# Indexer queries projected before keys, values and queries, and the indexer's scores dealt out among the eight query projections

## What is computed

```python
(u_h, u_b, u_c, z_a, q, k, v, qi, ki, wi, z_b, g_a, g_b) = _split_proj(h @ w_in)
q = _rms(q.reshape(b, t, N_HEADS, HEAD_DIM), q_norm)          # 8 heads of 128
k = _rms(k.reshape(b, t, N_KV_HEADS, HEAD_DIM), k_norm)       # 2 heads of 128
qi = qi.reshape(b, t, N_IDX_HEADS, IDX_DIM)                   # 8 indexer heads of 64

def _index_scores(qi, wi, kidx):
    s = jnp.einsum('btid,bsd->btis', qi, kidx) * (IDX_DIM ** -0.5)
    w = wi * (N_IDX_HEADS ** -0.5)
    return jnp.einsum('btis,bti->bts', jax.nn.relu(s), w)

sc = jnp.where(key_pos <= pos, _index_scores(qib, wib, kidx), NEG_INF)
_, idx = lax.top_k(sc, 256)
```

## Time and profile before

| | us |
|---|---|
| median of 3 runs | 3638.25 |
| lowest and highest run | 3633.06, 3639.53 |
| span of the profiled execution | 3631.9 |
| PE busy | 3443.6 (95%) |
| DVE busy | 2334.5 (64%) |
| ACT busy | 1497.9 (41%) |
| POOL busy | 1561.8 (43%) |

### The profile page before, as it was taken

How to read it: one execution, slowest core, us unless ns; L and a number is a source line. 1 busy time by engine, 2 the same in 40 slices (tenths; PEclk the granted TensorE clock), 3 DMA queues, 4 the chain that set the end, 5 groups by cost and what they waited for, 6 DMA issues and landing times.

```text
span 3631.9 us, 44594 instructions
## 1 busy us (share of the span) xinstructions
PE 3443.6 (95%) x16753; PEld 2772.4 (76%) x16753; DVE 2334.5 (64%) x3959; ACT 1497.9 (41%) x2452; POOL 1561.8 (43%) x1076
## 2 busy tenths in 40 slices
PE   7899999999899999999999999979999999997999
PEld 6779888855577778887777688868877588876887
DVE  2563599200263589953546999985555999997653
ACT  2344432332353354335533643334433744334532
POOL 2226564300154438753353287541263167650014
PEclk9999999988899999999999999989999999998999
DMA  7222223343334423342244133420144133440005
GB/s 202 73 82 86 60 70 99 99 166 136 100 99 122 117 65 97 104 134 60 75 144 118 38 95 100 128 78 13 46 146 126 33 85 95 114 127 9 10 13 160
DMA packets 520871, 338.02 MB, mean 93 GB/s; under 512 B 15405, under 2 KB 494823, under 8 KB 518610
## 3 DMA queue, kind: packets, MB, share of 16 engines
q1 hardware_dynamic: 517202, 297.41, 29.6%
q0 software_dynamic: 3456, 37.75, 2.8%
HBM read 296.36 MB, written 38.76 MB: 92 GB/s over the span
## 4 chain that ended last, share of the span: by engine, by line
PE 63%; DVE 26%; issue 5%; ACT 3%; POOL 2%; DMA 1%; SPq 1%; ACTq 0%; DVEq 0%; POOLq 0%
PE ps L982 58%; DVE JUNK L1635 12%; PE ps L987 5%; DVE GE L1637 1%; DVE SC L1577 1%; DVE SMALL L1641 1%; DVE SMALL L1639 1%; DVE PFX L1661 1%; DVE SMALL L1642 1%; DVE QI L1555 1%; DVE QI L1556 1%; ACT T L673 1%; DVE RS L1510 1%; DVE BD L1664 1%; DVE SC L1665 1%
## 5 line engine op out<-in xcount | busy, mean ns | idle before, releaser
L982 PE MATMUL ps<-HTH,WLH 128*128 128x512 f32 x4672 | 1480.4, 393 | 3.2 <-POOL WLH L1858 3.2
L1858 POOL TENSOR_TENSOR WLH<-WR,WLH 128x1024 fp32r<-128x1024 f32 x388 | 957.1, 2467 | 1161.2 <-ACT WLH L582 1161.0
L982 PEld LDWEIGHTS ps<-HTH,WLH 128*128 128x128 f32 x4672 | 880.1, 188 | 192.0 <-issue 6.5
L982 PE MATMUL ps<-HTL,WLH 128*128 128x512 f32 x2336 | 911.6, 390 | 0.0
L582 ACT ACTIVATE WLH<-WR 128x1024 fp32r<-128x1024 f32 x388 | 411.4, 1060 | 1032.0 <-DMA WR<-in_w_in 753.4
L1635 DVE TENSOR_SCALAR_CACHE_REDUCE JUNK<-SC,SMALL 128x384 bf16<-128x384 f32 (+13 forms) x392 | 579.9, 1479 | 25.6 <-POOL SC L1906 10.0
L982 PEld LDWEIGHTS ps<-HTL,WLH 128*128 128x128 f32 x2336 | 440.3, 188 | 94.3 <-issue 6.5
L1708 DVE CUSTOM_DVE_ANT_0 LP<-ps,SC 128x512 f32<-128x512 f32 (+3 forms) x320 | 187.5, 609 | 226.1 <-PE ps L982 223.4
L982 PE MATMUL ps<-T,V 128*128 128x256 f32 x1088 | 283.0, 388 | 5.8 <-ACT T L858 5.8
L982 PEld LDWEIGHTS ps<-T,V 128*128 128x128 f32 x1088 | 187.0, 191 | 34.4 <-ACT T L858 12.6
L1510 DVE RECIPROCAL RS<-RS 128x512 f32<-128x512 f32 x40 | 134.1, 3352 | 107.3 <-ACT RS L657 107.2
(11 more groups left out here) (314 smaller groups left out, 5417.4 us busy)
## 6 DMA issues: line engine op xcount, KB each, us to landing
WR<-in_w_in SPq DMA_DIRECT2D x292, 512.0 KB, 3.9
WR<-in_w_proj_a SPq DMA_DIRECT2D x32, 512.0 KB, 4.1
WR<-in_w_proj_b SPq DMA_DIRECT2D x32, 512.0 KB, 4.2
WR<-in_w_out SPq DMA_DIRECT2D x32, 512.0 KB, 4.3
MW<-in_w_mod SPq DMA_DIRECT2D x24, 512.0 KB, 7.2
XN<-in_x_prompt SPq DMA_DIRECT2D x4, 2048.0 KB, 9.4
q_scratch<-QO SPq DMA_DIRECT2D x32, 256.0 KB, 4.4
ma_scratch<-T SPq DMA_DIRECT2D x32, 256.0 KB, 4.4
```

The source lines that it names most:

```text
L982: return pe.matmul(out, lhsT, rhs, start=start, stop=stop, **more)
L1858: pool.tensor_tensor(WL[j % 3][:, :, :], WR[j % 3][:, :, :], WH[j % 3][:, :, :].bitcast(F32), ALU.subtract).then_inc(*w_split.mark(j))
```

## The change

`PROJ_A` is reordered to `ki`, 4 `qi`, 2 `k`, 2 `v`, 8 `q`. The index stage's units are cut into eight equal shares (`index_share`: 2, 8, 12 or 16 units in tiles 0 to 3), and share k is issued with query head k's projection: on PE behind the products of that projection (and behind `after_a` of the one ahead), on ACT behind `root_a` of the one ahead, on DVE in front of `item_a` of that head.

```diff
-PROJ_A = [("ki", 0)] + [("k", h) for h in range(KV)] + [("v", h) for h in range(KV)] \
-    + [("q", h) for h in range(HEADS)] + [("qi", i) for i in range(IH // 2)]
+PROJ_A = [("ki", 0)] + [("qi", i) for i in range(IH // 2)] + [("k", h) for h in range(KV)] \
+    + [("v", h) for h in range(KV)] + [("q", h) for h in range(HEADS)]
+QI_LAST = PROJ_A.index(("qi", IH // 2 - 1))
+Q_FIRST = PROJ_A.index(("q", 0))
...
+    def index_share(t, i):
+        units = [(b, h, c, n) for b in index_blocks(t) for h in range(IH) for c, n in pieces(width(BLOCKS * t + b))]
+        m, k = len(units), i - Q_FIRST
+        return units[m * k // HEADS:m * (k + 1) // HEADS] if k >= 0 else []
...
                 evac_a(t, i, j)
                 if i:
                     root_a(t, i - 1)
+                index_relu(t, i)
                 j += 1
             root_a(t, len(PROJ_A) - 1)
-            index_relu(t)
...
                 if i >= 2:
                     turn_keys(t, i - 2)
+                index(t, i)
                 j += 1
             after_a(t, len(PROJ_A) - 1, j - 1)
-            index(t)
...
             for i in range(len(PROJ_A)):
+                weigh(t, i)
                 item_a(t, i, j)
                 j += 1
-            weigh(t)
```

More of the change, by code:

```diff
@@ L660, in _, with index_relu @@
         relus = [0]
[L662 to L674, removed]
+        def index_relu(t, i):
+            if i == Q_FIRST:
+                act.wait_ge(*a_done.at(t, QI_LAST, last_part(t)))
+            for b, h, c, n in index_share(t, i):
+                r = relus[0]
+                relus[0] += 1
+                act.wait_ge(*idx_done.at(t, b, h, c))
+                if r >= 4:
+                    act.wait_ge(*scored.at(r - 4))
+                act.activation(T[1 + r % 4][:, 0:n], ps[bank("idx", t, b, h, c)][:, 0:n], ACT.Relu
+                               ).then_inc(*relu.mark(r))
         def conv_taps(f):
@@ L1136, in turn_keys, with index @@
                 freed[b] = a_done.at(t, i, p)
[L1138 to L1151, removed]
+        def index(t, i):
+            if i == Q_FIRST:
+                pe.wait_ge(*a_done.at(t, QI_LAST, "P"))
+            for blk, h, c, n in index_share(t, i):
+                b = aux("idx", t, blk, h, c)
+                q = QI[:, h, blk * P:(blk + 1) * P]
+                mm(ps[b][:, 0:n], q, KIH[:, c:c + n], True, False)
+                mm(ps[b][:, 0:n], q, KIL[:, c:c + n], False, True).then_inc(*idx_done.mark(t, blk, h, c))
+                freed[b] = relu.at(relus[0])
+                relus[0] += 1
         relus = [0]
@@ L1559, in _, with weigh @@
         relus = [0]
[L1561 to L1577, removed]
+        def weigh(t, i):
+            for blk, h, c, n in index_share(t, i):
+                r = relus[0]
+                relus[0] += 1
+                dve.wait_ge(*relu.at(r))
+                dst = scores(t)[:, blk, c:c + n]
+                x = T[1 + r % 4][:, 0:n]
+                w = WI[:, blk, h:h + 1]
+                if h == 0:
+                    dve.tensor_scalar(dst, x, w, None, ALU.mult).then_inc(*scored.mark(r))
+                else:
+                    dve.wait_ge(*scored.at(r - len(pieces(width(BLOCKS * t + blk)))))
+                    dve.scalar_tensor_tensor(dst, x, w, dst, ALU.mult, ALU.add).then_inc(*scored.mark(r))
         def sample_index():
```

## The result

| | before | after |
|---|---|---|
| median, us | 3635.65 (4 runs) | 3653.64 (4 runs) |
| lowest and highest run | 3632.99, 3639.53 | 3649.76, 3658.39 |
| span of the profiled execution | 3631.9 | 3652.7 |

The ratio after to before is 1.0049, 95% interval 1.0035 to 1.0064: the change makes the kernel slower, by 18 us or 0.5%. The time lies at the upper edge of the range (3654), but the forecast was 3640, no change, and that is wrong by 14.

What follows compares the result with a forecast made beforehand. PE was taken to bound tiles 0 and 1, DVE's path to select tiles 2 and 3. Terms -7.3 - 11 + 13 + 7 = +1.7 gave span 3633.6, median 3640 us, range 3626 to 3654.

Steps and rivals of the forecast that it cites:

- Tile 0, -7.3: Last projection to PROJ_B 7.3 us shorter: the 16 pairs now lie between projections, where nobody waits for them.
- Tile 1, -11: First projection's end to PROJ_B 126.0 us instead of 138.3, 12.3 less; with 1 for SP's queue, 11 earlier.
- Tile 1, SP's queue: PROJ_B's fourth load now stands behind the last head's store; two projections of cover make that cost 0 to 1.5, taken as 1.
- Tile 3, +7: First projection's end to select 186.9 us instead of 181.98, 4.9 later, plus 2 for half clock: 7 later.
- the four parts: Tile 3's chain to select: nine projections and first relu 55.5, weighings 75.4, seven turns 51.9, last head 4.1; sum 186.9 us.
- the turn: DVE's step from one share to the next, waiting for the head's root: 7.4 us, seven per tile in tiles 2 and 3.
- regain 1.4: After half clock costs PE 1.7 us in tile 3, its 8 units left regain 1.4 on DVE; 0.3 stays per turn.
- Tile 2, +13: First projection's end to select about 5.0 us longer, taken as 6, plus 7 for half clock: 13 later.
- Rival 1: Half clock lasts long, as in the 10.0 us case: 4 us a turn over 14 turns, 3687; chance 0.1.
- Rival 2: POOL's split wins against DVE's weighings; tile 1's step becomes 11.3 us against 9.6, giving 3652; chance 0.08.
- Rival 3: The clock does not fall in tiles 2 and 3; without those 9 us the time is 3631; chance 0.2.
- Rival 4: Root is ready when DVE ends its share; turns 4.13, tiles 2 and 3 each 18 us earlier, 3583; chance 0.05.

Runs made afterwards that it cites:

- e6_two_tiles: Changed kernel with shares in tiles 0 and 1 only, and SP's last store behind the load for PROJ_B's fourth projection: 3622.70 us, ratio to before 0.9963.
- e1: Changed kernel with SP's store of the last query head moved behind the load for PROJ_B's fourth projection: 3649.95 us, repeated 3648.17.
- e3_filler: Changed kernel with 12 unused matmuls on PE behind the 8th unit of every share in tiles 2 and 3: 3647.78 us, ratio to before 1.0047.
- e8_filler7: Changed kernel with 12 unused matmuls on PE in seven of eight shares of tiles 2 and 3, none in the first: 3636.50 us, ratio to before 1.0011.
- e4_both: Changed kernel with each DVE share ahead of the previous head's reciprocal, and SP's last two stores each behind one more PROJ_B load: 3587.41 us, repeated 3583.45.

## Why the prediction was right, and where it was wrong

- **What bounds which tile** was right: PE in tiles 0 and 1, DVE up to `select` in 2 and 3. e6_two_tiles gains with tiles 0 and 1 alone.
- **Tile 0, -7.3: the step that failed is the last of it, "nobody waits".** The 6.3 at `PROJ_B`'s start were there, and SP's held load took them. I had charged that load in tile 1 ("two projections of cover make it 0 to 1.5") and not at all in tile 0. The cover was counted for the load and its split alone, but ACT works in order: the copy that PE waits for stands behind the split. The stop cost 3.55, and half the clock for 10 us 2.9 more up to the third projection's start and 1.6 in that projection. At `BAH` 6.8 of it are left, mainly because the kernel before had its clock at half 3.4 us longer on the way there; e1 takes these 6.8 back. Off by 8.
- **Tile 1, -11:** `PROJ_B` came 129.1 after the first projection's end. The sum of nine projections (53.8 forecast, 53.8 measured) and the steps (9.6 and 9.55) held. Missing was the stop of 2.84 at the last share, and another 1.5 until `BAH` (181.0 from `PROJ_B`'s start, 179.5 before). That is the clock: e3_filler and e8_filler7 have the same stop in tile 1 (2.85 and 2.83), but in their profiles the clock stayed up behind it, and the stretch is 179.9 and 180.0. Behind that stop, in the changed kernel and then in e8_filler7 (columns as in the earlier trace rows):

```profile
1310.20:1313.60 3.40, 3.38 (x6) 2.08 (x7) 3.40 (x6) 3.03 (x5) 0.00 (x0) 0.50 0.02 7
```

```profile
1306.60:1311.60 5.00, 5.00 (x20) 3.78 (x21) 5.00 (x7) 3.19 (x5) 1.61 (x1) 1.00 0.00 1
```

- **Tile 1, SP's queue:** the 1 us charged for it was not paid here: with the load ahead of the store, e1 takes 182.3 and 181.6 for the same stretch, no less than the changed kernel. Tile 1 is off by 3 in all.
- **Tile 3, +7:** the four parts were 55.5, 75.4, 51.9 and 4.1, with 2 for the clock. Measured: 55.6, 75.0, 60.4 and 4.1. So the turn is the term that was mis-sized, 8.63 each instead of 7.4 and 0.3 for the clock. e8_filler7 parts it: 5.6 for the clock (forecast 2), and 2.9 that stay without it. Nearly all of these are PE's lead over DVE at the end of a share. I took 3.86 from the last units before, all 512 wide. In e8_filler7 DVE's idle falls from 4.14 at the first turn to 3.37 at the seventh, and the lead grows from 3.11 to 3.83 (3.49 on average, so 2.6 of the 2.9): in the first blocks each fourth unit is 128 wide, which DVE is through sooner. That the width is the reason is read from the order of units, no run varies it. That the units left "regain 1.4" was the error in the clock's sum: of the 1.7 that 3.4 us of half clock cost, 0.8 a turn stayed (5.6 over seven), not 0.3. Why so little is regained no run isolates.
- **Tile 2, +13:** the start of `select` came 14.7 later. The clock's 7 was 5.9; the turns' 6 was 8.8, mostly again the lead (3.28 on average in e8_filler7). The other 2 us lie behind `select`, and in after_again, another execution of the same kernel (tile 2: 843.2), they are not there.
- **Rival 1** (long half clock) did not come in tiles 2 and 3: stretches of 3.4, twice 6.8. The 10.0 us came in tile 0, where I had no stop. **Rival 2** gave the measured number, 3652, but not by its mechanism: tile 1's steps were 9.55, not 11.3. POOL's split and DVE's weighings beside it there:

```profile
1273.11 2.79 POOL L1859 TENSOR_TENSOR WLH<-WR,WLH 128x1024 fp32r<-128x1024 f32 x1 [7.06 <-ACT WLH L590]
...
1269.31 4.32 DVE L1578 SCALAR_TENSOR_TENSOR SC<-T,WI,SC 128x512 f32<-128x512 f32 x8
```

- This split began 0.5 us before the weighings ended and took 2.79 instead of 2.39: POOL waited. All the weighings of tiles 1, 2 and 3 were busy for 35.0, 55.2 and 75.6 us, against 34.7, 55.0 and 75.1 before, so the splits among them cost DVE at most half a us a tile. **Rival 3** (no dips) is out: the clock fell after 11 of 14 stops. **Rival 4** (the root is there, turns of 4.13, 3583) was not this change, but it named the repair: e4_both gets 3587 and 3583 by one line of DVE's order and two stores.
- **The range held by luck.** Its upper edge, 3654, was drawn to take in rival 2 (3652), whose mechanism did not come; the measured 3653.64 got there by the held load, the stop in tile 1, the lead and the clock.
- **The chances:** slower had 0.27. The range allowed half a us a turn either way. In truth two terms (the held load, the last share's stop) left out a wait and the lead was taken at its longest, and all three can only be off towards slower.

## What to carry to other kernels

When work is dealt out among steps, look on each engine at what now stands between an instruction and its input: here the reciprocal for a head was issued right behind a share, and its root came a whole projection later, while the root of the head before had long been there; delaying it by one share was worth 25 us in each of two tiles. When a load moves behind a store in a queue, follow it to the engine that splits or copies its data, and to what stands behind that instruction in order. And take a lead between two engines from the first of the units concerned as well as from the last.

## What the runs showed of the hardware

Stops of PE of 2.5 to 3.2 us, once per head, were followed by 3.4 us or more at half the clock in 11 of 14 cases, and filling them with matmuls that nobody uses kept the granted clock at 1.00 and made the kernel faster: a ratio to the kernel before of 1.0011 instead of 1.0049, with 168 matmuls more. The same stop is not always followed by half the clock: in tile 1 one of 2.84 us was, for 3.4 us, in both profiles of the changed kernel, and one of 2.83 and 2.85 us at the same place in e8_filler7 and e3_filler was not. One stop of 3.55 us in tile 0, with small matmuls and transposes behind it, was followed by 10 us at half the clock.
